# Two gated recurrences, with heads laid over the partitions and the two directions as planes

## Chip, core and metric

The kernel runs on one core of a Trainium2 chip. The metric is the device time of one launch in microseconds (us). The engines are called as the profile calls them: PE (the matrix engine; PEld is its weight load), DVE (vector), ACT (scalar), POOL and SP.

## What is computed

Two transformer blocks over 512 positions of width 1024, in fp32. The change touches the first block's mixers alone. Three mixers read one projection of the input: differential attention (a), a gated recurrence with four heads of 64 keys (b), and one with four heads of 32 keys (c). Both recurrences run forward and backward and are summed:

```python
def chunk_scan(q, k, v, log_a):
    # S_t = diag(a_t) S_{t-1} + k_t v_t^T,  o_t = S_t^T q_t, chunkwise
    ...
        cum = jnp.cumsum(ac, axis=2)
        o_inter = jnp.einsum('bhtk,bhkv->bhtv', qc * jnp.exp(cum), state)
        diff = cum[:, :, :, None, :] - cum[:, :, None, :, :]
        scores = jnp.einsum('bhtk,bhsk,bhtsk->bhts', qc, kc, decay)   # decay = exp(diff), causal
        o_intra = jnp.einsum('bhts,bhsv->bhtv', scores, vc)
        new_state = jnp.exp(last[:, :, 0, :])[..., None] * state + jnp.einsum(
            'bhsk,bhsv->bhkv', kc * jnp.exp(last - cum), vc)
...
def bidir_scan(q, k_fwd, k_bwd, v, la_fwd, la_bwd):
    fwd = chunk_scan(q, k_fwd, v, la_fwd)
    bwd = flip(chunk_scan(flip(q), flip(k_bwd), flip(v), flip(la_bwd)))
    return (fwd + bwd).astype(q.dtype)
```

In b the keys of the two directions differ (one minus the forget gate of each), in c they are the same.

## The kernel before

Positions lie on the free axis (512 columns), features on the partitions. Large matmuls run as three of a split pair: weights are cut by ACT (`WH`) and POOL (`WL`) into two parts, the input into `HHI` and `HLO`, and each tile of weights costs three matmuls of 512 columns. Each engine runs one instruction list in its given order; semaphores alone tie the lists together. For the mixers, all five lists come from one list of steps, `P.steps`. The planner's `placed` merges five streams by a start and a gap, both counted in rows of the projection stream: `projections` (25 units of weights, 8 rows each, six matmuls of 512 columns in a plain row), `decays` of b, `recurrences` (start 8, gap 1.1) and `attention` (start 75, gap 1.7). An engine picks its own part out of every step.

There are six recurrence scans. Two are c's (two heads each), four are b's (one head each). The 128 partitions of a scan hold, for each head, the forward keys and then the backward keys. So queries and keys of every head are copied by small DMAs to the partitions of both directions (`QKC`, on SP's queue, lines 669 to 676; `QKB`, on ACT's queue, `copies`). Inside a chunk of 128 positions the scores are built in eight levels. On level lv, blocks of 2m positions (m = 64 halved lv times) are cut in the middle, and only pairs across the middle are right; a mask picks them. The steps of a level:

- `differ` (DVE, line 2191): running sum of log decay less its value at the block's middle, into `DD`, 512 elements a partition
- `expo` (ACT, lines 1574 to 1578): four exponentials of 256 elements. The first two write the query's factors and take a bias from `SC` that makes one direction zero
- `scale` (DVE, line 2199): multiplies queries and keys by them, 1024 elements
- `product` (PE, line 981): keys times queries for each of four chunks, c into banks 4 and 5 (two heads of 64 rows), b into bank 4 (one head of 128 rows)
- `collect` (DVE, lines 2208 and 2213): the bank's 512 scores into `SCT`, masked from level 1 on. The next product into the bank waits for it (`free`, `holds`)

`DD` has two buffers, so `differ` of a level waits for the product two levels back. Between the levels of a scan stand the steps that carry the state from chunk to chunk: `ends` and `reach_k` (factors and keys, `KH`), `turn` (four transposes into bank 6), an eviction into `KN` by ACT, `state` (bank 6), `carry` (DVE, `ST`, lines 2241 to 2245, chain by direction and head) and `read` (bank 7, scores times values plus state times queries). The norm of an output pair then takes the step `mean` (PE, bank 6) and a logarithm on ACT that frees the bank.

Of the kernel before, what the change touches and what calls it, by code (L numbers as in the profile page):

```python
# [24 lines left out]
DECAY, RECUR, ATTEND = ((16, 2), (34, 2.2)), (8, 1.1), (75, 1.7)  # L25
LEVELS = [(r, lv) for r in range(6) for lv in range(7)]
# [57 lines left out]
def unit_order():  # L84
# [14 lines left out]
    for d, (tag, n) in enumerate(DENSE):  # L99
        if tag == "bz":  # L100
            c = []
            for h in (2 * n, 2 * n + 1):
                c += [(1792 + 64 * h, 64), (2048 + 64 * h, 64)]
# [51 lines left out]
def unit_size(u):  # L155
# [6 lines left out]
       ("sgnh", 1), ("sgnc", 1), ("fh", 1), ("bh", 1), ("fc", 1), ("bc", 1),  # L162
# [70 lines left out]
class Plan:  # L233


    def __init__(self):
# [7 lines left out]
        for u in self.units:  # L244
# [8 lines left out]
        self.slots()  # L253
        self.steps = placed((self.projections(), (0, 1)), (self.decays(0), DECAY[0]), (self.decays(1), DECAY[1]),
                            (self.recurrences(), RECUR), (self.attention(), ATTEND))
# [30 lines left out]
    def place(self):  # L286
# [3 lines left out]
        for d, (tag, n) in enumerate(DENSE):  # L290
            if d == 9:
                self.turn = 0
            self.take(four if d < 9 else [3, 5], (at[tag, n], 0), (at[tag, n], 1))
# [41 lines left out]
    def projections(self):  # L335

        late, later, copies = [], [], []
        for tag, n in DENSE:
# [14 lines left out]
            for m in range(2):  # L353
                for row in range(4):
                    r = 4 * m + row
                    step = [("nat", i, m, row // 2)] * (row % 2 == 0) if natural else [("gemm", i, m, 2 * row)]
                    yield step + beside[r] + (late if row == 1 else []) + (later if row == 2 else []) + (copies if row == 3 else [])
                late = [("evict", i, tag, n, m)]
                later = [("silu", i, tag, m)] if tag in ("cg", "bg", "bq") else []
                copies = [("copies", m)] if tag == "bq" else []  # L360
# [6 lines left out]
    def recurrences(self):  # L367
# [4 lines left out]
        box = {0: ("c", 0), 1: ("c", 1), 3: ("b", 0), 5: ("b", 1)}  # L372
# [4 lines left out]
        for r in range(6):  # L377
            for k in range(8):
                g = 7 * r + k
                one, two, three = [("product", r, k)], [], []  # L380
                if k < 7 and g + 1 < len(LEVELS):
                    two.append(("scale", *LEVELS[g + 1]))
                if k < 7 and g + 2 < len(LEVELS):
                    two.append(("differ", *LEVELS[g + 2]))
                    three.append(("expo", *LEVELS[g + 2]))
                if k == 0 and r:
                    two.insert(0, ("read", r - 1))
                elif k == 1:
                    one.append(("ends", r))
                elif k == 2:  # L390
                    three.append(("turn", r))
                elif k == 3:
                    two.append(("state", r))
                elif k == 4:
                    one.append(("carry", r))
                    one.append(("eq", r))
                elif k == 5 and r < 5:
                    one.append(("lag", r + 1))
# [2503 lines left out]
```

## Time and profile before

| | us |
|---|---|
| median of 3 runs | 2272.03 |
| lowest and highest | 2271.94, 2275.05 |
| the profiled execution | 2274.05 |
| its span in the profile | 2272.3 |

The recurrences run between about 60 and 460 us of the span. A line of the timeline is one instruction or several equal ones in a row; a matmul of plain fp32 operands is recorded as two passes, so x8 is four matmuls. A wait is the idle time of an engine just before an instruction, with what ended it. PEclk is the share of full clock granted to PE: 1.00 is 2.4 GHz, 0.50 is 1.2 GHz.

### The profile page before, as it was taken

How to read it: one execution, taken by the hardware profiler on the slowest of the kernel's cores; microseconds unless marked ns; L12 is line 12 of the kernel's file. 1: busy time of each engine (PE TensorE's matmuls, PEld its weight loads, DVE VectorE, ACT ScalarE, POOL GpSimd, SP SyncE). 2: the span in 40 equal slices, each digit the busy share in tenths (PEclk: the TensorE clock that was granted, in tenths of full speed). 3: DMA queues.
4: the chain of work that ended last, by engine and by line, in shares of the span. 5: the costliest groups of instructions: out<-in, count | busy, mean ns of one | idle time of the engine just before them, and what ended most of it. 6: DMA issues, size and time to landing. Idle time of an engine off the chain costs nothing.

```text
span 2272.3 us, 29053 instructions
## 1 busy us (share of the span) xinstructions
PE 2220.5 (98%) x11592; PEld 1848.7 (81%) x11592; DVE 1150.9 (51%) x1864; ACT 998.5 (44%) x1888; POOL 1051.0 (46%) x794
## 2 busy tenths in 40 slices
PE   7899999999999999999999999999999999999998
PEld 4788777778988888888888888878888889888887
DVE  4887777736532122477672425431534446725353
ACT  4765566654533223566632322453322336322234
POOL 2544443446454444633454445544444444554444
PEclk9999999999999999999999999999999999999999
DMA  7222233464222232321223222322222222322321
GB/s 285 93 81 106 95 119 130 157 227 181 94 93 93 93 112 93 95 75 57 75 93 111 84 102 93 111 93 93 86 100 93 75 93 78 109 93 84 104 108 58
DMA packets 42663, 239.41 MB, mean 105 GB/s; under 512 B 5024, under 2 KB 7200, under 8 KB 17184
## 3 DMA queue, kind: packets, MB, share of 16 engines
q1 hardware_dynamic: 40096, 232.28, 28.9%
q10 hardware_dynamic: 2432, 5.27, 0.8%
q8 instruction: 92, 1.51, 0.3%
q14 instruction: 43, 0.35, 0.0%
HBM read 225.99 MB, written 8.39 MB: 103 GB/s over the span
## 4 chain that ended last, share of the span: by engine, by line
PE 81%; DVE 11%; ACT 4%; POOL 1%; issue 1%; DMA 1%; DVEq 0%; SPq 0%; ACTq 0%; POOLq 0%
PE PS L741 80%; DVE DD L1890 2%; POOL WL L2641 1%; DVE TG L1896 1%; DVE SQ L1896 1%; PE PS L1165 1%; DVE SCT L2213 1%; ACT WH L1316 1%; DVE HLO L1896 1%; DVE VV L1893 0%; DVE SB L2267 0%; DVE SB L1896 0%; DVE T L1890 0%; DVE PS L1896 0%; DVE X L1890 0%
## 5 line engine op out<-in xcount | busy, mean ns | idle before, releaser
L2641 POOL TENSOR_TENSOR WL<-RAW,WH 128x512 fp32r<-128x512 f32 (+1 forms) x688 | 924.0, 1372 | 1101.0 <-ACT WH L1316 1089.7
L741 PE MATMUL PS<-HHI,WH 128*128 128x512 f32 x1488 | 596.4, 401 | 1.5 <-DVE GB L1896 1.4
L741 PE MATMUL PS<-HHI,WL 128*128 128x512 f32 x1488 | 581.9, 391 | 0.0
L741 PE MATMUL PS<-HLO,WH 128*128 128x512 f32 x1488 | 581.4, 391 | 0.0
L1316 ACT ACTIVATE WH<-RAW 128x512 fp32r<-128x512 f32 (+1 forms) x688 | 378.3, 613 | 392.3 <-PE PS L741 376.5
L741 PEld LDWEIGHTS PS<-HHI,WH 128*128 128x128 f32 x1488 | 280.6, 189 | 72.5 <-issue 10.0
L741 PEld LDWEIGHTS PS<-HHI,WL 128*128 128x128 f32 x1488 | 280.3, 188 | 59.7
L741 PEld LDWEIGHTS PS<-HLO,WH 128*128 128x128 f32 x1488 | 280.7, 189 | 56.8 <-issue 2.4
L741 PE MATMUL PS<-UF,WH 128*128 128x512 f32 (+1 forms) x832 | 224.0, 357 | 0.0
L1890 DVE TENSOR_TENSOR T<-PS,R 128x512 f32<-128x512 f32 x112 | 76.9, 690 | 218.1 <-PE PS L741 210.2
L741 PEld LDWEIGHTS PS<-UF,WH 128*128 128x128 f32 x832 | 148.3, 189 | 22.8
L741 PE MATMUL PS<-UP,WH 128*128 128x512 f32 x512 | 157.6, 389 | 0.0
L1890 DVE TENSOR_TENSOR Y<-PS,Y 128x512 f32<-128x512 f32 (+1 forms) x97 | 66.3, 686 | 170.8 <-PE PS L741 170.7
L741 PE MATMUL PS<-UF,WL 128*128 128x512 f32 (+1 forms) x416 | 148.3, 356 | 0.0
L1834 ACT ACTIVATE TG<-TG 128x512 f32<-128x512 f32 x44 | 27.8, 632 | 206.3 <-DVE TG L1896 206.3
L741 PEld LDWEIGHTS PS<-UP,WH 128*128 128x128 f32 x512 | 96.1, 188 | 20.1
L741 PE MATMUL PS<-WH,HHI 128*128 128x256 f32 (+1 forms) x320 | 110.9, 347 | 0.2 <-ACT VV L1852 0.2
L741 PE MATMUL PS<-WL,HHI 128*128 128x256 f32 (+1 forms) x320 | 108.7, 340 | 0.0
L741 PE MATMUL PS<-WH,HLO 128*128 128x256 f32 (+1 forms) x320 | 108.7, 340 | 0.0
L1896 DVE SCALAR_TENSOR_TENSOR X<-PS,MOD,X 128x512 f32<-128x512 f32 (+1 forms) x56 | 37.0, 673 | 141.0 <-PE PS L741 141.0
L1896 DVE SCALAR_TENSOR_TENSOR TG<-T,V,TG 128x511 f32<-128x511 f32 x88 | 104.1, 1183 | 3.1
L741 PE MATMUL PS<-UP,WL 128*128 128x512 f32 x256 | 99.6, 389 | 0.0
(360 smaller groups left out, 3492.7 us busy)
## 6 DMA issues: line engine op xcount, KB each, us to landing
RAW<-in_wts SPq DMA_DIRECT2D x190, 1024.0 KB, 4.8
FW<-in_wts SPq DMA_DIRECT2D x6, 1024.0 KB, 17.4
spill<-T SPq DMA_DIRECT2D x24, 256.0 KB, 3.2
RAW<-in_wts SPq DMA_DIRECT2D x8, 768.0 KB, 4.2
GT<-spill SPq DMA_DIRECT2D x20, 256.0 KB, 4.9
X<-in_xt SPq DMA_DIRECT2D x2, 1024.0 KB, 9.1
out_x<-X SPq DMA_DIRECT2D x8, 256.0 KB, 2.3
X<-in_xt SPq DMA_DIRECT2D x2, 768.0 KB, 8.1
```

The lines of the kernel that those rows point to most:

```text
L741: return e.matmul(o_, l, r, start=start, stop=stop)
L1165: t = e.transpose(PS[:, 2 + part, 128 * s:128 * s + 128], S[:, s, 128 * part:128 * part + 128], ident)
L1316: e.activation(WH[i][:, cs], RAW[i % 2][:, cs], ACT.Copy).then_inc(*up("w_hi", ("w_hi", i, p)))
L1834: e.activation(G, G, ACT.Gelu_apprx_tanh).then_inc(*up("a_ev", ("gelu", name, j)))
L1890: return e.tensor_tensor(o_, a, b, f)
L1896: return e.scalar_tensor_tensor(out=o_, in0=a, scalar=s, in1=b, op0=f1, op1=f2)
L2213: t = e.copy_predicated(SCT[n][:, :].rearrange("p (c t) -> p c t", c=4), mk, PS[:, b, :].rearrange("p (c t) -> p c t", c=4))
L2641: return e.tensor_tensor(o_, a, b, f)
```

## The change

The partitions of a scan now hold heads alone, and the two directions are two planes of the free axis. Scan 0 is all four heads of c (32 rows each, `PAIRS` 2: its products come in two pairs), scans 1 and 2 are two heads of b each (64 rows, one pair). The running sums lie in `Am` as two planes, backward and forward. On a level each position is a query in one direction and a key in the other, so `differ` writes both halves by two instructions of 512 elements, and all of `DD` is used: no factor is set to zero, and one product serves both directions. Level 7, the diagonal, now uses the sum of both keys. Each product writes banks 4 and 5; `turn` writes banks 4 and 5, `state` bank 4, `mean` bank 5. The DMAs for `QKC` and `QKB` are gone. The c scan keeps start 8 and gap 1.1, the two b scans start at row 65 with gap 2.2.

```diff
-DECAY, RECUR, ATTEND = ((16, 2), (34, 2.2)), (8, 1.1), (75, 1.7)
-LEVELS = [(r, lv) for r in range(6) for lv in range(7)]
+DECAY, RECUR, ATTEND = ((16, 2), (34, 2.2)), ((8, 1.1), (65, 2.2)), (75, 1.7)
+LEVELS = [(r, lv) for r in range(3) for lv in range(8)]
+PAIRS = (2, 1, 1)
...
-        for m in range(2):
-            q.wait_ge(*at(("ev", U["cqk", 0], m)))
-            for n in range(8):
-                r, c = 64 * (n // 2 % 2) + 32 * (n % 2), 32 * (n // 2)
-                t = e.dma_start(QKC[r:r + 32, n // 4, m, :], T0[m][c:c + 32, :])
...
         # tensor_program: product
-            for n in range(len(heads)):
-                free(product_bank(r, n))
+            for i in range(2):
+                free(4 + i)
             for c in range(4):
                 cs = slice(128 * c, 128 * c + 128)
-                for n, (r0, nr, _, _) in enumerate(heads):
-                    t = mm(PS[:, product_bank(r, n), cs], both[r0:r0 + nr, 1, cs], both[r0:r0 + nr, 0, cs], True, True)
+                for i in range(2):
+                    rs = slice(nr * (2 * j + i), nr * (2 * j + i) + nr)
+                    t = mm(PS[:, 4 + i, cs], D[rs, 1, cs], D[rs, 0, cs] if lv < 7 else planes[rs, 0, cs], True, True)
...
         # tensor_program: turn
-            free(6)
-            for c in range(4):
-                t = e.transpose(PS[:, 6, 128 * c:128 * c + 128], KH[:, 128 * c:128 * c + 128], ident)
+            for d in range(2):
+                free(4 + d)
+                for k in range(3):
+                    t = e.transpose(PS[:, 4 + d, 128 * k:128 * k + 128], KH[:, d, 128 * k:128 * k + 128], ident)
...
         # scalar_program: expo
-            e.activation(Q[:, :, 0:m], K[:, :, 0:m], ACT.Exp, scale=-s, bias=SC[:, b[0]:b[0] + 1])
-            e.activation(Q[:, :, m:2 * m], K[:, :, m:2 * m], ACT.Exp, scale=s, bias=SC[:, b[1]:b[1] + 1]).then_inc(*up("a_mix", ("expo_q", r, lv)))
-            q.wait_ge(*at(("expo_q", r, lv)))
-            e.activation(K[:, :, 0:m], K[:, :, 0:m], ACT.Exp, scale=-s)
-            e.activation(K[:, :, m:2 * m], K[:, :, m:2 * m], ACT.Exp, scale=s).then_inc(*up("a_mix", ("expo", r, lv)))
+            e.activation(halves(D, lv, 0), halves(D, lv, 0), ACT.Exp, scale=-s)
+            e.activation(halves(D, lv, 1), halves(D, lv, 1), ACT.Exp, scale=s).then_inc(*up("a_mix", ("expo", r, lv)))
...
         # vector_program: differ, scale
-            tt(blocks(level(r, lv)[:, 1, :], lv), blocks(Am[:, :], lv), ref, SUB).then_inc(*up("d_mix", ("differ", r, lv)))
+            tt(halves(D, lv, 0), halves(sums, lv, 0), middle, SUB)
+            tt(halves(D[:, ::-1, :], lv, 1), halves(sums, lv, 1), middle, SUB).then_inc(*up("d_mix", ("differ", r, lv)))
...
-            tt(D, both, D, MUL).then_inc(*up("d_mix", ("scaled", r, lv)))
+                if r == 0:
+                    t = tt(D, planes, D, MUL)
                 else:
+                    tt(halves(D, lv, 0), halves(planes[:, 0:2, :], lv, 0), halves(D, lv, 0), MUL)
+                    t = tt(halves(D, lv, 1), halves(planes[:, 0:3:2, :], lv, 1), halves(D, lv, 1), MUL)
...
         # vector_program: carry
-            for n, (r0, nr, _, _) in enumerate(heads):
-                hf = nr // 2
-                for d, (s, c) in enumerate(((slice(r0, r0 + hf), [0, 1, 2, 3]), (slice(r0 + hf, r0 + nr), [3, 2, 1, 0]))):
-                    e.memset(ST[s, c[0], :], 0.0)
-                    e.tensor_copy(ST[s, c[1], :], S3[s, c[0], :]).then_inc(*up("d_mix", ("chain", r, n, d, 1)))
+            e.tensor_copy(ST[:, 0:6:5, :], S[:, 0:6:5, :]).then_inc(*up("d_mix", ("chain", r, 0)))
+            for k in (1, 2):
+                q.wait_ge(*at(("chain", r, k - 1)))
+                stt(ST[:, k, :], ST[:, k - 1, :], TD[:, k:k + 1], S[:, k, :], MUL, ADD)
+                n = 5 - k
+                t = stt(ST[:, n, :], ST[:, n + 1, :], TD[:, n + 2:n + 3], S[:, n, :], MUL, ADD)
```

The order of the carry on DVE, first scan. Before, the last two of its four chains (two heads, two directions), and the decays' step after them (`G`, of b's first half):

```order
L2241 MEMSET ST 32x64
L2242 COPY ST<-PS 32x64
L1896 SCALAR_TENSOR_TENSOR ST<-ST,TD,PS 32x64 x2
L2241 MEMSET ST 32x64
L2242 COPY ST<-PS 32x64
L1896 SCALAR_TENSOR_TENSOR ST<-ST,TD,PS 32x64 x2
L1896 SCALAR_TENSOR_TENSOR G_90<-G_90,LB,G_91 128x512 x2
```

After, the same place: the whole carry is two rows, and it stands right behind `differ` and `collect` of the same level; b's second half of decays stands around it:

```order
L1867 TENSOR_TENSOR ZB<-ZB,G_91 128x1024
L1867 TENSOR_TENSOR DD_107<-Am 128x512
L1867 TENSOR_TENSOR DD_107<-Am 128x2x256
L2189 COPY_PREDICATED SCT_110<-MASK,PS 128x1024
L2209 COPY ST<-PS 128x2x64
L1873 SCALAR_TENSOR_TENSOR ST<-ST,TD,PS 128x64 x4
L2276 COPY VB<-PS 128x512
L1873 SCALAR_TENSOR_TENSOR G_90<-G_90,LB,G_91 128x512 x2
```

What moved: sixteen rows' worth of chains of 32 partitions became five instructions over all 128, and the carry came behind a `collect`.

PE, from the transposes of the first scan to the next product. Before:

```order
L1003 MATMUL PS<-V,KH 128x128 x4
L741 MATMUL PS<-HHI,WH_66 128x512
L741 MATMUL PS<-HLO,WH_66 128x512
L741 MATMUL PS<-HHI,WL_68 128x512
L741 MATMUL PS<-HHI,WH_66 128x512
L741 MATMUL PS<-HLO,WH_66 128x512
L741 MATMUL PS<-HHI,WL_68 128x512
L741 MATMUL PS<-DD_107 128x128 x8
```

After:

```order
L994 MATMUL PS<-V,KH 128x128 x6
L732 MATMUL PS<-HHI,WH_66 128x512
L732 MATMUL PS<-HLO,WH_66 128x512
L732 MATMUL PS<-HHI,WL_68 128x512
L732 MATMUL PS<-HHI,WH_66 128x512
L732 MATMUL PS<-HLO,WH_66 128x512
L732 MATMUL PS<-HHI,WL_68 128x512
L732 MATMUL PS<-DD_107 128x128 x8
```

The distance is the same six matmuls; but the transposes now lie in the product's own banks, so the last row waits for the eviction into `KN` between them.

ACT, the exponentials of a level and that eviction. Before:

```order
L1574 ACTIVATE DD_106<-DD_106,SC 128x64x4
L1575 ACTIVATE DD_106<-DD_106,SC 128x64x4
L1577 ACTIVATE DD_106<-DD_106 128x64x4
L1578 ACTIVATE DD_106<-DD_106 128x64x4
L1607 ACTIVATE KN<-PS 128x512
```

After, with the decays' `G` and the eviction of b's queries ahead of it:

```order
L1531 ACTIVATE G_89<-ZB 128x1024
L1533 ACTIVATE G_89<-G_89 128x1024
L1645 ACTIVATE QKB<-PS 128x512
L1564 ACTIVATE DD_108<-DD_108 128x256x2
L1565 ACTIVATE DD_108<-DD_108 128x256x2
L1595 ACTIVATE KN<-PS 128x768
```

Four exponentials became two of twice the size, and `KN` grew from 512 to 768 elements.

## Rows read from the trace of the kernel before

**Rows 1.** Busy time by engine in two stretches, granted clock, DMA; first the columns
```profile
core 0: us, PE busy (x) PEld busy (x) DVE busy (x) ACT busy (x) POOL busy (x), PEclk, DMA share, GB/s
60.00:180.00 120.00, 107.64 (x775) 92.45 (x775) 101.87 (x145) 84.70 (x152) 59.57 (x35) 0.94 0.26 86
180.00:460.00 280.00, 268.23 (x1503) 215.36 (x1502) 213.93 (x342) 170.75 (x355) 119.30 (x78) 0.99 0.35 125
```

**Rows 2.** PE's waits, 60 to 180 us: total, times, longest
```profile
PE PS L741 <- DVE SCT L2213: 10.2, 2, 6.1
PE PS L741 <- DVE Am L2183: 2.1, 1, 2.1
```

**Rows 3.** PE's waits, 180 to 460 us, the longest total
```profile
PE PS L741 <- DVE SCT L2213: 3.1, 3, 2.5
```

**Rows 4.** Timeline of PE after its longest wait: start, us, instruction, idle before
```profile
113.75 2.08 PE L741 MATMUL PS<-DD 64*128 64x128 f32 x16 [6.08 <-DVE SCT L2213]
...
118.91 0.63 PE L741 MATMUL PS<-HLO,WH 128*128 128x512 f32 x1
119.34 0.58 PE L741 MATMUL PS<-HHI,WL 128*128 128x512 f32 x1
```

**Rows 5.** Timeline of PE around a product of c
```profile
133.89 0.39 PE L741 MATMUL PS<-HHI,WL 128*128 128x512 f32 x1
134.21 1.16 PE L741 MATMUL PS<-DD 64*128 64x128 f32 x16
135.30 0.50 PE L741 MATMUL PS<-HHI,WH 128*128 128x512 f32 x1
135.64 0.39 PE L741 MATMUL PS<-HLO,WH 128*128 128x512 f32 x1
```

**Rows 6.** Timeline of PE around a product of b
```profile
272.32 0.39 PE L741 MATMUL PS<-HLO,WH 128*128 128x512 f32 x1
272.54 0.39 PE L741 MATMUL PS<-HHI,WL 128*128 128x512 f32 x1
272.77 1.05 PE L741 MATMUL PS<-DD 128*128 128x128 f32 x8
273.58 0.48 PE L741 MATMUL PS<-HHI,WH 128*128 128x512 f32 x1
273.89 0.40 PE L741 MATMUL PS<-HLO,WH 128*128 128x512 f32 x1
```

**Rows 7.** Timeline of PE, state times queries, one of c and one of b
```profile
137.92 1.09 PE L741 MATMUL PS<-KH,ST 64*64 64x128 f32 x16
...
390.88 1.04 PE L741 MATMUL PS<-KH,ST 128*64 128x128 f32 x8
```

**Rows 8.** DVE's groups by form, 60 to 460 us: busy, mean ns | idle before
```profile
L1890 DVE TENSOR_TENSOR DD<-QKB,DD 128x1024 f32<-128x1024 f32 x28 | 41.7, 1489 | 4.1 <-ACT DD L1578 4.1
L2213 DVE COPY_PREDICATED SCT<-MASK,PS 128x512 f32<-128x512 uint8 x56 | 39.4, 730 | 2.5 <-PE PS L741 2.4
L1890 DVE TENSOR_TENSOR DD<-Am,ZB 128x512 f32<-128x512 f32 x28 | 29.1, 1039 | 9.9 <-PE PS L741 8.0 <-ACT Am L1564 1.8
```

**Rows 9.** ACT's groups by form, 60 to 460 us
```profile
L1574 ACT ACTIVATE DD<-DD,SC 128x256 f32<-128x256 f32 x42 | 21.4, 510 | 48.0 <-DVE DD L1890 47.9
L1577 ACT ACTIVATE DD<-DD 128x256 f32<-128x256 f32 x42 | 17.8, 425 | 1.3
L1629 ACT ACT_TABLE_LOAD x7 | 9.0, 1283 | 0.1
L1563 ACT ACTIVATE Am<-ZB 64x512 f32<-64x512 f32 x4 | 2.5, 619 | 0.0
```

**Rows 10.** Timeline of DVE, the first scan's carry: its first instruction, and the next step
```profile
103.25 0.11 DVE L2241 MEMSET ST<- 32x64 f32 x1
...
107.23 2.20 DVE L1896 SCALAR_TENSOR_TENSOR G<-G,LB,G 128x512 f32<-128x512 f32 x2
```

**Rows 11.** Timeline of PE, the first scan's transposes
```profile
94.05 0.60 PE L1003 MATMUL PS<-V,KH 128*128 128x128 f32 x4
```

**Rows 12.** Timeline of ACT, the first scan's eviction into KN
```profile
95.83 0.57 ACT L1607 ACTIVATE KN<-PS 128x512 f32<-128x512 f32 x1
```

More of the change, by code:

```diff
@@ L335, in projections @@
     def projections(self):
-        late, later, copies = [], [], []
+        late, later = [], []
         for tag, n in DENSE:
@@ L376, in recurrences @@
         yield [("scale", 0, 0), ("expo", 0, 1)]
[L377 to L381, printed above, removed]
+        for g, (r, k) in enumerate(LEVELS):
+            for j in range(PAIRS[r]):
+                last = j + 1 == PAIRS[r]
+                one, two, three = [("product", r, k, j)], [], []
+                if (r, k) == (2, 0):
+                    two.append(("read", 1, 0))
+                if j == 0 and g + 1 < len(LEVELS):
@@ L391, in recurrences @@
                     three.append(("turn", r))
[L392 to L395, printed above, removed]
+                elif last and k == 4:
                     one.append(("eq", r))
-                elif k == 5 and r < 5:
-                    one.append(("lag", r + 1))
-                if k == 1:
-                    three.append(("reach_k", r))
-                if k == 5:
-                    two.append(("reach_q", r))
@@ L403, in recurrences @@
-                if k > 3 and r - 1 in box:
-                    three.append(("norm", *box[r - 1], k - 4))
-                two.append(("collect", r, k))
+                    three.append(("state", r))
+                    three.append(("carry", r))
+                elif last and k == 5:
+                    two.append(("reach_q", r))
+                    if r < 2:
+                        three.append(("lag", r + 1))
+                elif last and (r, k) == (0, 7):
+                    one.append(("read", 0, 0))
@@ new lines, in recurrences @@
+                two.append(("collect", r, k, j))
+                for at_, step in {(1, 0): ((one, 0), (three, 1), (three, 2)), (1, 1): ((one, 3),), (1, 2): ((one, 4), (three, 5), (three, 6)),
+                                  (1, 3): ((two, 7),), (2, 0): ((three, 8),), (2, 1): ((three, 9), (three, 10)),
+                                  (2, 2): ((two, 11),)}.get((r, k), ()):
+                    at_.append(("norm", *(("c", 0), ("c", 1), ("b", 0))[step // 4], step % 4))
+                if (r, k) == (1, 1):
+                    three.append(("read", 0, 1))
@@ L1013, in state @@
+            for n in range(6):
+                d, k = divmod(n, 3)
+                for i in range(128 // nr):
+                    t = mm(PS[nr * i:nr * i + nr, 4, 64 * n:64 * n + 64], KN[:, d, 128 * k + nr * i:128 * k + nr * i + nr],
+                           vals[:, k + d, vc + 64 * i:vc + 64 * i + 64], True, True)
             t.then_inc(*up("psum", ("state", r)))
-            holds(6, ("carry", r))
-        def read(r):
-            _, _, heads, vals, _, _, _, _, _ = scan(r)
+            holds(4, ("carry", r))
@@ L1595, in ends_q @@
         def ends_q(r):
+            s = scan(r)[5]
             q.wait_ge(*at(("turn", r)))
[L1598 removed]
+            e.activation(KH[:, 0, :], FWD[:, 128:512], ACT.Exp, scale=s)
+            for c in range(3):
                 cs = slice(128 * c, 128 * c + 128)
[L1600 removed]
+                t = e.activation(KH[:, 1, cs], BWD[:, cs], ACT.Exp, scale=-s, bias=SC[:, 12 + c:13 + c])
             t.then_inc(*up("a_mix", ("eq", r)))
```

318 lines of the change are left out of this document (137 added, 181 removed).

## The prediction, made before the run

> **What bounds the kernel now.** I read the busy time by stretch first, then who PE waited for, then the timeline at those waits. PE is the bound: in the recurrences it is busy 107.6 of 120 us and 268.2 of 280 us [rows 1], and outside them the change touches nothing. So only three things can give time: the 24.1 us that PE stands idle there (12.4 and 11.8), the clock it loses after a stand, and PE's own work. The waits say whose fault the idle time is. In the first stretch it is DVE alone: 10.2 us for `collect` (line 2213), 2.1 us for a small memset [rows 2]. DVE is busy 101.9 of 120 us there [rows 1], so it is not one slow step but a queue that is full. In the second stretch `collect` is 3.1 us [rows 3], and the rest of the 11.8 us is spread over waits of attention's and the norms' steps, mostly on DVE, which is busy 76% there [rows 1].
>
> A stand costs more than itself. After the wait of 6.08 us the matmuls of 512 columns follow each other at 0.43 us (118.91 to 119.34) [rows 4], where elsewhere it is 0.23 us (272.32 to 272.54) [rows 6]: the clock is at 1.2 GHz in place of 2.4. That lasts to 119.6 or so, 6 us of work at half pace, some 2.6 us lost. The mean clock of the two stretches, 0.94 of 120 us and 0.99 of 280 us [rows 1], makes 7.2 and 2.8 us of clock not granted; part of it fell into idle time. I take 8 us as the price of the clock.
>
> **PE's own work.** The cost of a product is what it adds to the pace of its neighbours. A product of c: from the matmul ahead of it to the second one behind, 135.64 - 133.89 = 1.75 us, less two paces of 0.227 us: 1.30 us, for eight matmuls on 64 rows [rows 5]. One of b: 273.89 - 272.54 = 1.35, less 0.45: 0.90 us, for four matmuls on 128 rows [rows 6]. So sixteen passes on half the rows take 1.09 us where eight on all rows take 0.81: pairs on two row halves run at the same time, and the entry and exit cost a little more. Before there are 16 products of c and 32 of b: 16 x 1.30 + 32 x 0.90 = 49.6 us. After there are 32, all of eight matmuls in pairs: 32 x 1.30 = 41.6 us. That is 8 us less. Half of them are on quarters of the rows (32), which no row shows; at worst the two quarters do not overlap, and a product costs twice the four matmuls of b, 1.80 us: 16 x 0.5 = 8 us more, and this gain is gone. At best they cost what the halves cost; the order gives PE only two quarters at a time, so not less. I take 1.30, since the mechanism is the same.
>
> The Trainium skill ("TensorEngine Tiling (Array Packing)", Restrictions and Gotchas) says that different row tiles cannot access the same PSUM bank simultaneously. State times queries of c does just that, two row halves into bank 7, and its sixteen passes take 1.09 us where b's eight on all rows take 1.04 [rows 7]: the trace does not agree for this case. By the page's rule each of the four new reads would be some 1.4 us longer, 5.6 us in all; by the row it is nothing.
>
> The rest of PE: 24 transposes become 18, four of them took 0.60 us [rows 11], so 0.6 to 0.7 us less with their entries. States: 32 matmuls in six groups become 48 in three, reads: 64 in six groups become 80 in four. Matmuls in pairs cost about 0.13 us each (1.09 us for eight [rows 7]), and a group's entry and exit is about 0.2 us: 16 more matmuls of state at 0.08 (half the columns) against three entries and the unpaired four of b, about -0.8 us; reads 4 x 2.8 against 2 x 2.25 + 4 x 2.1, about -1.8 us. Sum of PE's own work: -8 - 0.7 - 0.8 - 1.8 = **-11.3 us**. All of this is on the path, since PE is.
>
> **DVE.** `scale`: 42 instructions of 1024 elements at 1.49 us [rows 8] (c's are alike) become 7 of 1024 and, in b, 28 of 512 at 1.04 us, plus three additions of 512: 62.6 becomes 10.4 + 29.1 + 3.1, 20 us less. `differ`: 42 of 512 before, 42 of 512 after, at 1.04 us [rows 8]: nothing. `collect`: 64 of 512 at 0.73 us [rows 8] become 32 of 1024; per element it must read as much, and only the fixed part is saved, about 2.5 us. `carry`: the four chains of c take 107.23 - 103.25 = 3.98 us [rows 10], b's two chains half; 2 x 4 + 4 x 1.9 = 15.6 us become three times one copy and four multiply-adds, some 1.3 us: 11.6 us less. `ends`: six instructions' worth of small work each becomes one, 2.5 us less. Together 36 us of 315.8 [rows 1]. In the first stretch it is 10 (scale) + 1.3 + 6.7 + 0.9, 19 us of 101.9: DVE's share falls from 85 to 70%.
>
> **ACT.** `expo`: 42 x (2 x 0.51 + 2 x 0.42) = 78 us [rows 9] become 21 x 2 of 512 elements without a bias, 0.62 us by the copy of that size [rows 9]: 26 us, 52 less. The factors of `KH` and the copies of `Am` save another 14. ACT had 255 us [rows 1], so it was no bound; the gain is that a level's chain, `differ`, `expo`, `scale`, is a microsecond shorter, and that ACT's queue is seldom late. POOL's `reach` shrinks by a quarter. The small DMAs stood on queues that nobody waited for: nothing.
>
> **What becomes of the waits.** The 6.08 us wait ends a stretch in which DVE has no idle time; it now has at least 6 us less to do there (a scale and four carry chains), so I take this wait as gone. The 4.1 us one has the decays of b's second half ahead of it, 10 us in a row on DVE. They still stand there, so 1 to 3 us stay. The memset is gone with its 2.1 us. In the second stretch `collect` mostly goes, and of the 8.7 us of others a third, as DVE falls to about 70%.
>
> Three kinds of wait are new, because bank 6 is given up. (1) After `turn`, the next product waits for `KN`: before, `KN` ended at 96.40 [rows 12], 1.8 us behind the transposes' end [rows 11], and six matmuls at 0.23 are 1.4 us; with a wider `KN` and a shorter `expo` ahead some 0.8 us in c, nothing in b, where more stands between. Behind the waiting product everything on PE is queued, the projections too. (2) After `state`, the next product waits for the carry, 1.3 us and DVE's queue; `state` itself waits for the `collect` of its own level. I take 3.5 us in c (with the rest of the 4.1 us above) and 1 us in each b scan. The bound from above is what the trace shows: `state` was done at 99.3 and the carry at 107.2 [rows 10], 8 us later. (3) After `mean` in bank 5 the next product waits for the logarithm, a table load of 1.28 us [rows 9] and 0.7 us, with twelve matmuls or 2.7 us as cover: 0.7 us each for three outputs. Together 8.3 us new, 4.3 us old: 12.6 in place of 24.1, **-11.5 us**. Of the clock's 8 us I take half, as short waits remain: **-4 us**.
>
> Sum: -11.3 - 11.5 - 4 = -26.8 us. The profiled execution took 2274.05 us, 2.0 us above the median of the runs; the sum on the execution is 2247.3, and on the median 2245.2. I say **2245**.
>
> **Rivals.** *All cover holds*: no new wait shows and DVE is never late. Then 11.3 + 24.1 less about 2 + 8 = 41 us go: 2231. For it speaks DVE's share of 70%; against it the lumps of the decays. *The waits only change their name*: the order decides, not the load, and each wait removed comes back at a shared bank. Then PE's own work is left: 2261. *Quarters do not pair*: the change does not do on PE what it does for the halves: 2245 + 8 = 2253. *Slower*: the shared banks. Nine places (`KN`, carry and logarithm, three each) put PE behind another engine's queue. The trace shows 1.8 and 8 us for the first two. If each costs over 4 us net, that is 36 us and eats all that the change gives (11.3 + 17 + 8); at 5.5 us it is 49.5 us, and with the clock's half pace after the longer ones 2286. Against it speaks that both queues get shorter, and that in b the steps stand twice as far apart.
>
> **Chances.** Forecast 0.55, all cover 0.15, name change 0.13, quarters 0.07, slower 0.06, and 0.04 that it cancels within 0.2%. The range 2230 to 2262 takes in the first four. A measurement can tell about 0.2%, 4.5 us: faster 0.89, same 0.05, slower 0.06.
>
> **What would show it.** Products of 16 passes on 32 and 64 rows at 1.1 us with 1.30 us added; PE idle 12 to 13 us between 60 and 440 us, in waits of under 3 us; the wait of 6 us gone; at most two stretches at 1.2 GHz; DVE near 280 and ACT near 190 us over the recurrences; waits of a product on `KN`, `ST` and the logarithm, each near 1 us. It is wrong if the waits at banks 4 and 5 add up to over 15 us, if the quarters' products cost 1.8 us, or if DVE's instructions with two planes and short blocks run longer than those of the same size before.

## The result, and the profile after

The changed kernel takes 2276.93 us (median of 18 runs, 2275.04 to 2278.47), the one before beside it 2272.43 us (18 runs, 2269.92 to 2275.07): a ratio of 1.0018, with an interval of 1.0012 to 1.0025. That is 4.5 us slower: small, just the size that the prediction called the least that can be told, but with an interval that does not reach 1. 2245 was forecast, and 2276.9 lies outside the range of 2230 to 2262. The profiled execution took 2276.7 us. Of all executions reported here one is left out, of `before_split`: it ran at a mean granted clock of 0.75 and took 2754.97 us.

Busy time by stretch comes first, as in [rows 1]: PE, PEld, DVE, ACT and POOL, the granted clock, DMA.

```profile
60.00:180.00 120.00, 111.40 (x800) 95.58 (x800) 95.85 (x94) 64.91 (x96) 62.02 (x38) 0.95 0.20 69
180.00:460.00 280.00, 260.28 (x1541) 201.18 (x1541) 193.14 (x278) 128.38 (x244) 107.92 (x74) 0.95 0.35 125
```

Over 60 to 460 us, ACT went from 255.5 to 193.3 us, as forecast (190). DVE went from 315.8 to 289.0, 27 us less where 36 were forecast (280), and in the first stretch it lost only 6.0 us where 19 were: its share is 80% there, not 70%. In the first stretch PE stands idle 8.6 us instead of 12.4. In the second, where the prediction let most waits of before go and added small ones, it stands idle 19.7 us instead of 11.8, and the granted clock there fell from 0.99 to 0.95. Who PE waited for, 60 to 180 us and then 180 to 460 (total, times, longest), against [rows 2, 3]:

```profile
PE PS L732 <- DVE SCT L2189: 6.4, 4, 2.7
PE PS L732 <- DVE ST L1873: 1.4, 1, 1.4
```
```profile
PE PS L732 <- DVE T L1873: 4.9, 2, 2.9
PE PS L1046 <- DVE SB L1873: 4.0, 1, 4.0
PE PS L732 <- DVE SCT L2189: 3.7, 1, 3.7
PE PS L732 <- DVE SQ L1873: 3.0, 1, 3.0
PE PS L732 <- ACT T L1608: 3.0, 1, 3.0
```

The 6.1 us wait and the memset's 2.1 are gone. In their place stand many waits of 2 to 4 us, and in the second stretch most of them are not on the recurrences at all: `SB` is the attention's tile, `T` the norms', and `SQ` a sum that DVE makes for the modulation. The timeline of PE at three of the longer ones shows the price of each (start, duration, instruction, idle before it):

```profile
238.43 1.12 PE L1046 MATMUL PS<-V,SB 128*128 128x128 f32 x4 [3.96 <-DVE SB L1873]
239.20 0.78 PE L732 MATMUL PS<-HHI,WH 128*128 128x512 f32 x1
239.78 0.63 PE L732 MATMUL PS<-HLO,WH 128*128 128x512 f32 x1
240.20 0.63 PE L732 MATMUL PS<-HHI,WL 128*128 128x512 f32 x1
```
```profile
376.41 1.85 PE L732 MATMUL PS<-V,SQ 128*128 128x1 f32 x8 [2.98 <-DVE SQ L1873]
378.12 1.52 PE L994 MATMUL PS<-V,KH 128*128 128x128 f32 x6
```
```profile
146.87 0.88 PE L732 MATMUL PS<-VC,KN 128*32 128x64 f32 x48 [2.68 <-DVE SCT L2189]
149.18 2.08 PE L732 MATMUL PS<-DD 32*128 32x128 f32 x16 [1.43 <-DVE ST L1873]
```

Behind the wait at 238.43, matmuls of 512 columns follow each other at 0.42 us (239.78 to 240.20), where [rows 6] have 0.23: 1.2 GHz in place of 2.4. The product at 149.18 takes 2.08 us, where 1.16 is the rule, as in [rows 4]. Over four short stretches the granted clock reads as follows:

```profile
112.00:132.00 20.00, 17.74 (x100) 13.67 (x100) 15.54 (x20) 11.70 (x21) 10.77 (x8) 0.91 0.30 106
144.00:160.00 16.00, 11.89 (x132) 11.06 (x131) 12.64 (x17) 7.05 (x11) 4.43 (x4) 0.79 0.21 68
232.00:248.00 16.00, 12.04 (x50) 9.07 (x49) 13.32 (x24) 4.93 (x10) 6.55 (x5) 0.79 0.36 131
372.00:384.00 12.00, 9.02 (x37) 7.62 (x37) 4.51 (x6) 3.91 (x8) 1.36 (x1) 0.72 0.52 193
```

To see what went where, I took the same four numbers from every trace: PE's idle time between 56 and 600 us (604 for before_tight, whose head starts later); the stretches at 1.2 GHz in it; what they cost (half of the part of them that was not idle); and the start of the first matmul of the mlp's head, which is preceded by an idle 0.53 us in every kernel. The last of them less idle time and clock is PE's own work, with a constant that is the same for all. The kernels below "after" are the experiments of the next section.

| kernel | median us | idle | at 1.2 GHz (stretches) | clock lost | head starts | own work |
|---|---|---|---|---|---|---|
| before | 2272.4 | 25.5 | 20.5 (5) | 9.8 | 591.0 | 555.7 |
| after | 2276.9 | 32.0 | 44.4 (10) | 20.4 | 593.4 | 541.0 |
| norm_late | 2264.8 | 27.2 | 27.3 (6) | 12.5 | 580.4 | 540.7 |
| state7 | 2270.3 | 31.5 | 27.3 (8) | 13.7 | 587.0 | 541.8 |
| scale_one | 2275.0 | 34.4 | 37.5 (8) | 16.4 | 591.4 | 540.6 |
| both | 2258.5 | 23.7 | 13.7 (3) | 6.7 | 573.7 | 543.3 |
| both_shift | 2256.2 | 22.1 | 23.9 (5) | 11.1 | 575.2 | 542.0 |
| both_coll | 2255.4 | 23.1 | 13.7 (3) | 5.8 | 571.8 | 542.9 |
| both_attn | 2257.9 | 22.7 | 27.3 (6) | 13.5 | 577.7 | 541.5 |
| before_split | 2276.2 | 27.5 | 20.5 (5) | 9.5 | 593.5 | 556.5 |
| before_late | 2271.9 | 24.6 | 27.3 (5) | 11.0 | 590.7 | 555.1 |
| before_tight | 2286.4 | 35.5 | 37.5 (7) | 14.4 | 604.0 | 554.1 |

So the change does save PE's own work, and more than forecast: 555.7 to 541.0, 14.7 us. It pays back 6.5 us in waits and 10.6 in clock, 2.4 us more than it saved. Of the profiled execution's 2.7 us more span, 2.4 are there by the head of the mlp. The column "own work" agrees within 2.7 us for the changed kernel and the seven made from it, and within 2.4 for the kernel before and the three made from it, so the split can be trusted to about that.

The columns after the median are of one execution each, and the clock's depends on more than the edits. In both, behind a wait of 1.89 us at 146.5 us, there is no stretch at 1.2 GHz; in both_shift and both_attn, behind waits of 1.91 and 1.88 us at the same place, there is one of 6.8 us, 3.4 us lost. The profiled executions of these two are 2.2 and 3.0 us above their medians. That the change costs clock at all is in every execution: the mean granted clock is 0.989 to 0.991 in the 18 of the changed kernel and 0.993 to 0.996 in those of the kernel before it.

### The profile page after: what moved, and what is told of

Same layout as the page of the kernel before. It is cut to its first block, busy times and chain, and to the rows that moved or that the text cites. A ratio compares the mean times of both kernels' runs of the same rounds, so it can differ in the third digit from the quotient of the medians.

```text
span 2275.0 us, 28817 instructions
## 1 busy us (share of the span) xinstructions
PE 2216.9 (97%) x11650; PEld 1837.9 (81%) x11650; DVE 1125.6 (49%) x1747; ACT 937.6 (41%) x1722; POOL 1042.6 (46%) x794
## 4 chain that ended last, share of the span: by engine, by line
PE 84%; DVE 9%; ACT 4%; POOL 1%; issue 1%; DMA 1%; ACTq 0%; DVEq 0%; SPq 0%; POOLq 0%
PE PS L732 83%; DVE DD L1867 2%; POOL WL L2607 1%; PE PS L1162 1%; DVE SQ L1873 1%; ACT WH L1313 1%; DVE HLO L1873 1%; DVE VV L1870 0%; DVE SCT L2189 0%; DVE TG L1873 0%; DVE PS L1873 0%; DVE X L1867 0%; DMA X<-in_xt 0%; DVE SB L1873 0%; ACT SB L1630 0%
## 5 line engine op out<-in xcount | busy, mean ns | idle before, releaser
L732 PEld LDWEIGHTS PS<-UF,WH 128*128 128x128 f32 x832 | 148.3, 189 | 22.7
```

Source lines behind the costliest of these rows:

```text
L732: return e.matmul(o_, l, r, start=start, stop=stop)
```

## Why PE waits: three theories, and the runs that tell them apart

**Theory 1, the head of DVE's line at the norms.** In the order before, the square, the mean, the logarithm with the multiply, and the copy of a norm stood one level apart. In the changed order, for three of the norms, the mean (step 1) and step 2, which is ACT's logarithm and exponential and then DVE's multiply, are due in one entry. DVE reaches its multiply before ACT has begun, and stands at it with everything behind it. DVE's timeline ahead of the wait at 238.43 shows it:

```profile
223.05 0.75 DVE L1873 SCALAR_TENSOR_TENSOR SQ<-RAW,CC,SQ 128x512 f32<-128x512 f32 x1
230.54 0.75 DVE L1873 SCALAR_TENSOR_TENSOR T<-PS,V,R 128x512 f32<-128x512 f32 x1 [6.74 <-ACT R L1620]
231.21 0.74 DVE L1873 SCALAR_TENSOR_TENSOR SQ<-RAW,CC,SQ 128x512 f32<-128x512 f32 x1
231.87 0.68 DVE L2235 CUSTOM_DVE_ANT_0 SB<-PS,MC 128x512 f32<-128x512 f32 x1
...
236.75 1.63 DVE L1873 SCALAR_TENSOR_TENSOR SB<-SB,SC,SB 128x512 f32<-128x512 f32 x1
```

ACT's, in the same time:

```profile
226.49 1.28 ACT L1617 ACT_TABLE_LOAD   x1
227.78 0.69 ACT L1617 ACTIVATE R<-PS,EPSC 128x512 f32<-128x512 f32 x1
228.49 1.28 ACT L1620 ACT_TABLE_LOAD   x1
229.78 0.72 ACT L1620 ACTIVATE R<-R,EPSC 128x512 f32<-128x512 f32 x1
```

DVE stands 6.74 us for `R`. The attention's logits (line 2235) are queued behind it, ACT's softmax behind those, then the division and `SB` again on DVE, and at the end PE's four transposes, 3.96 us late. The chain crosses three engines before PE notices.

**Theory 2, the shared bank of the states.** `state` writes into bank 4, which the level's own product holds until DVE has collected it. At 146.87 PE waits 2.68 us for that, and then 1.43 us more for the carry.

**Theory 3, DVE in lumps.** b's `scale` is two instructions in place of one, and a level's collect stands behind `scale` and `differ`. DVE ahead of the wait at 376.41, under GpSimd's `WL`:

```profile
368.72 3.48 DVE L1867 TENSOR_TENSOR DD<-QKB,DD 128x512 f32<-128x512 f32 x2
372.13 2.38 DVE L1867 TENSOR_TENSOR DD<-Am 128x512 f32<-128x512 f32 x2
374.43 1.29 DVE L2189 COPY_PREDICATED SCT<-MASK,PS 128x1024 f32<-128x1024 uint8 x1
375.62 0.73 DVE L1873 SCALAR_TENSOR_TENSOR SQ<-RAW,CC,SQ 128x512 f32<-128x512 f32 x1
```

### norm_late: DVE's part of the norms behind ACT's

DVE's and GpSimd's part of each norm becomes a step of its own (4), one entry later for the three outputs inside the recurrences; for b's last and the attention's it stays in the entry of step 2. The copy of step 3 moves one or two entries later with it. By the traces PE's order stays the same. DVE's multiply goes behind seven instructions at the second of the three norms, among them the attention's logits, and behind three at the third; at the first it passes nothing. ACT's copies (`OC`, `OB`) move too, and no run moves them alone.

```diff
-{(1, 0): ((one, 0), (three, 1), (three, 2)), (1, 1): ((one, 3),), (1, 2): ((one, 4), (three, 5), (three, 6)), ...
-at_.append(("norm", *(("c", 0), ("c", 1), ("b", 0))[step // 4], step % 4))
+{(1, 0): ((one, 0), (three, 1), (three, 2)), (1, 1): ((one, 4), (three, 3)), (1, 2): ((one, 5), (three, 6), (three, 7)), ...
+at_.append(("norm", *(("c", 0), ("c", 1), ("b", 0))[step // 5], step % 5))
...
-            if step == 2:
+            if step == 4:
                 q.wait_ge(*at(("r", kind, n)))
```

> The changed kernel, with the vector part of each norm (DVE's multiplication by 1/rms and what follows it) one or two steps of its stream behind ACT's logarithm and exponential. Theory 1, head of line: DVE's queue stands at that multiplication until ACT has gone through two table loads (DVE idle before T 23.6 + 7.5 us between 60 and 480 us), the softmax of attention queued behind it is late, and PE waits for SB or T. Then DVE's idle time before T falls below 15 us, PE's waits for T and SB (11.9 us) fall by 6 us or more, the stretches at 1.2 GHz lose two, and the time falls by 6 to 12 us, to 2265 to 2271. Theory 2, shared banks 4 and 5: PE's waits are at the state and the products, nothing of them goes, time within 3 us of the changed kernel (2274 to 2280). Theory 3, DVE's work in lumps: the same as theory 2.

Measured: 2264.84 us (2263.80 to 2267.34), 0.9973 of the kernel before (0.9961 to 0.9984), 12.1 us under the changed kernel. The same piece of DVE's timeline now reads:

```profile
224.68 0.69 DVE L2235 CUSTOM_DVE_ANT_0 SB<-PS,MC 128x512 f32<-128x512 f32 x1 [0.63 <-PE PS L732]
...
229.98 0.75 DVE L1873 SCALAR_TENSOR_TENSOR T<-PS,V,R 128x512 f32<-128x512 f32 x1 [1.99 <-ACT R L1620]
```

The logits stand ahead of the norm's multiply, begin at 224.7 instead of 231.9, and PE's wait there is 0.52 us instead of 3.96. DVE still waits for `R`, but nothing that is urgent stands behind it. Theory 1 holds: the time fell to just under its range, though one of its signs was weaker (DVE's waits for `R` fell to 16.9 us, not below 15). By the table 4.8 us of the gain are idle time and 7.9 are clock. At the wait of 238.43 alone 3.4 us of idle time and a stretch with 2.5 us lost are gone. But two stretches, 3.4 us lost in all, are also gone behind waits that kept their length (1.98 and 1.97 us at 290 and 284 us, 1.89 and 1.87 at 471 and 458), so part of the 12 us is where such stretches happen to fall.

### state7: the states in a bank of their own

```diff
-            free(4)
+            free(7)
...
-            holds(4, ("carry", r))
+            holds(7, ("carry", r))
```

(and bank 7 in the matmuls and in the carry's read.)

> The changed kernel, with the state matmuls of a scan in bank 7 in place of bank 4, so that the state no longer waits for the collect of its level and the next product no longer for the carry. Theory 2, shared banks: the waits of the state (2.7 and 3.7 us) and of the product behind the carry (1.4 us) go, with the half clock that follows two of them, together 8 to 12 us: 2265 to 2269. Theory 1, head of line at the norms: the 7.8 us of these waits go or turn up at the next product's collect, the rest of PE's waits stays, time falls by 0 to 5 us. Theory 3, DVE in lumps: the state no longer waits but the next product does, for the same collect: under 3 us.

Measured: 2270.31 us (2268.07 to 2272.01), ratio 0.9990 (0.9981 to 0.9999), 6.6 us under the changed kernel: less than the 8 to 12 us that theory 2 gave and more than the 0 to 5 of theory 1. The waits of 2.68 and 3.74 us at the two states are gone. PE's idle time fell only from 32.0 to 31.5: at 147 us a wait of 1.87 and at 402 us one of 1.89 come instead, and a wait for the attention's norm at 355 us grew from 2.88 to 4.47. But the stretches at 1.2 GHz fell from 44.4 to 27.3 us, the clock lost from 20.4 to 13.7.

Only 1.0 us of these 6.7 is at a state: two stands in a row, 2.68 and 1.43 us with 0.88 us of matmuls between them, became one, and the stretch behind them went from 6.8 to 3.4 us. The rest is at places whose waits the edit did not shorten. Behind the 3.96 us at 235 us the stretch is 3.4 us where it was 6.8; behind the 2.93 us at 372 us likewise; behind the 2.97 us at 344 and the 1.87 at 464 us there is none where there was one. The gain is in all eleven executions (mean granted clock 0.991 to 0.993, against 0.989 to 0.991), so it is real. That the states' own waits are what brings it is not shown.

### scale_one and before_split: the lumps

One takes b's second `scale` instruction away in the changed kernel, and leaves b's backward keys out of its scores by that; the other puts it into the kernel before.

```diff
-                    tt(halves(D, lv, 0), halves(planes[:, 0:2, :], lv, 0), halves(D, lv, 0), MUL)
-                    t = tt(halves(D, lv, 1), halves(planes[:, 0:3:2, :], lv, 1), halves(D, lv, 1), MUL)
+                t = tt(D, planes[:, 0:2, :], D, MUL)
```
```diff
-            tt(D, both, D, MUL).then_inc(*up("d_mix", ("scaled", r, lv)))
+                for hf in range(2):
+                    a, b = [... the blocks' half hf of D and of both ...]
+                    t = tt(a, b, a, MUL)
```

> The changed kernel, with b's scale as one instruction of 1024 elements in place of two of 512 (it takes the forward keys for both directions, so the backward keys are left out of b's scores on levels 0 to 6). Theory 3, DVE in lumps: under POOL's weight splits two short instructions take 3.48 us where one long took 2.3, fourteen times; then DVE loses some 10 us of work (28 x 1.17 against 14 x 1.5), the waits at 376 and 397 us shrink by over 1 us each, time falls by 4 to 8 us. Theories 1 and 2: time falls by under 3 us, since the waits come from the order and not from DVE's load.

> The kernel before, with each of the 28 scales of b as two instructions of 512 elements (same result). Theory 3, DVE in lumps: DVE gets 28 x (2 x 1.17 - 1.49), 24 us more work, where it is the bound of the waits, and the time rises by 6 us or more, to over 2278. Theories 1 and 2: the time rises by under 4 us.

Measured: scale_one 2274.99 us (2268.55 to 2276.30), 1.9 us under the changed kernel, ratio to before 1.0007 (0.9998 to 1.0016); before_split 2276.22 (2275.43 to 2277.49), ratio 1.0019 (1.0010 to 1.0028), 3.3 us above the kernel before beside it (2272.91). The second is clear of noise; the first isn't, as its interval meets the changed kernel's (1.0012 to 1.0025). So the split has a price of some 2 to 4 us, which the prediction did not have: there 20 us less of DVE's `scale` were counted at nothing either way, being off the path. The waits at the states and norms do not hang on it: in scale_one they are 2.67, 3.65 and 3.99 us (2.68, 3.74 and 3.96 in the changed kernel).

Both runs test theory 3 less hard than was meant. DVE's groups over 60 to 460 us, in before_split:

```profile
L1890 DVE TENSOR_TENSOR DD<-QKB,DD 128x512 f32<-128x512 f32 x56 | 51.8, 965 | 5.5 <-ACT DD L1578 5.3
L1890 DVE TENSOR_TENSOR DD<-Am,ZB 128x512 f32<-128x512 f32 x28 | 24.7, 882 | 8.4 <-PE PS L741 6.6 <-ACT Am L1564 1.7
```

Splitting added 10.1 us to `scale` (41.7 in [rows 8]), not 24, while `differ` lost 4.4 (29.1 in [rows 8]); all of DVE went from 315.8 to 316.6 us only. In scale_one `scale` lost 9.4 us, `differ` gained 7.7, and all of DVE went from 289.0 to 285.9. So they show what the number of instructions costs, and not what 24 us of load would.

### before_tight and before_late: the same edits in the kernel before

If theory 1 is right, the order before must become slow in the same way when its norms are drawn together. PE's order is the same in this kernel. By the traces DVE's multiply stands 4, 8 and 15 instructions earlier at the three norms (not two to four, as the expectation has it), and ACT's table loads, logarithm and exponential move up with it.

```diff
-                if k > 3 and r - 1 in box:
-                    three.append(("norm", *box[r - 1], k - 4))
+                if r - 1 in box:
+                    three += [("norm", *box[r - 1], n) for n in {4: (0,), 5: (1, 2), 6: (3,)}.get(k, ())]
```

> The kernel before with the norms of its recurrences drawn together as the change has them: the mean and the step with logarithm, exponential and multiply in one step, the square and the copy where they would then fall; nothing else is changed (TensorE's row order is the same, VectorE's multiply stands two to four instructions earlier). If the head of VectorE's line at the norms is what the change added, it is slower by 3 to 10 us: 2275 to 2282, with VectorE's waits for R up from 14.2 by 8 us or more. If the banks or the lumps of VectorE's work are the cause, it stays at 2271 to 2274.

> The kernel before with the norm's edit alone: VectorE's and GpSimd's part of each norm as a step of its own behind ScalarE's. In the kernel before the mean already stands a level ahead of ScalarE's logarithm, but VectorE's multiply in the same step as ScalarE's two table loads, and VectorE waited 14.2 us for R. If the cost in the changed kernel came from drawing the mean and that step together (23.6 us of waits for R there), little is to be had here: 2270 to 2273. If every place where VectorE reaches the multiply in the same step costs alike, it gains 3 to 8 us: 2264 to 2269.

Measured: before_tight 2286.36 us (2284.82 to 2286.98), ratio 1.0058 (1.0045 to 1.0070), 12.9 us slower than the kernel before beside it, where theory 1 gave 3 to 10. before_late 2271.91, ratio 0.9996 (0.9987 to 1.0005): no change. DVE and then PE of before_tight:

```profile
245.98 0.75 DVE L1896 SCALAR_TENSOR_TENSOR T<-PS,V,R 128x512 f32<-128x512 f32 x1 [7.18 <-ACT R L1632]
246.64 0.74 DVE L1896 SCALAR_TENSOR_TENSOR SQ<-RAW,CC,SQ 128x512 f32<-128x512 f32 x1
...
248.82 1.63 DVE L1896 SCALAR_TENSOR_TENSOR SB<-SB,SC,SB 128x512 f32<-128x512 f32 x1
```
```profile
250.51 1.11 PE L1049 MATMUL PS<-V,SB 128*128 128x128 f32 x4 [8.53 <-DVE SB L1896]
```

The same signature, in a kernel without a single one of the change's other parts: DVE 7.2 us at the norm's multiply, the softmax's last steps behind it (the logits are ahead of it here), and a wait of 8.5 us at the attention's transposes. With the stretch of 10.2 us at 1.2 GHz around it (2.6 us lost), this one place has 11.2 of the 12.9 us; in the kernel before PE has no wait there. And DVE's waits for `R` over 60 to 480 us, in before, after, before_tight and before_late:

```profile
DVE T L1896 <- ACT R L1632: 14.2, 4, 5.1
```
```profile
DVE T L1873 <- ACT R L1620: 23.6, 4, 7.9
```
```profile
DVE T L1896 <- ACT R L1632: 22.6, 4, 7.2
```
```profile
DVE T L1898 <- ACT R L1634: 7.3, 2, 4.2
```

Up by 8.4 us costs 12.9 us; down by 6.9 us brings nothing. The total of an idle time on DVE is no measure: in the kernel before, the longest of the four (5.13 us, at 249.72) stands behind the softmax and the collect of its level, and no step of the attention is among the next three behind it.

### both, and the start moved by one: do the gains add?

> The changed kernel with both edits at once: VectorE's and GpSimd's part of each norm as a later step of its own, and the states with their carries in bank 7. If the two causes are separate (the head of VectorE's line at the norms, and the states that wait for a collect in bank 4), their gains of 12.1 and 6.6 us add: 2258.2, range 2255 to 2262, with TensorE's waits of 2.71 and 3.7 us at the states and of 3.96 us at the transposes of the attention gone together, and less than 25 us at 1.2 GHz between 56 and 600 us. If both only move one shared slack (a stream that is late waits at its next partner anyway), the gains overlap and it comes at 2262 to 2265, no better than the norm's edit alone.

> The kernel with both edits, and the start of the second stream of recurrences one step later (66 in place of 65), so that everything from the second scan on meets the stages' own steps and the attention elsewhere; no work is changed. If the time lies in the two named causes, which are gone here, it stands within 2 us of the kernel with both edits. If it lies in where short waits happen to fall (and what stretches at 1.2 GHz they bring), it may go 3 to 8 us either way, and the gains of the two edits have that uncertainty on them too.

Measured: both 2258.53 us (2256.38 to 2260.16), ratio 0.9935 (0.9923 to 0.9948). The sum of the two gains had given 2258.2, and overlapping gains 2262 to 2265. The gains of the two edits add, in time; where the clock's part of them comes from is as open as above. both_shift (the second stream's start, 65, is 66): 2256.20 (2254.36 to 2258.41), 2.3 us less, with other waits at other places (5.2 us at one of them). That is between the under 2 us and the 3 to 8 us that were expected. So how the streams happen to meet is worth 2 us or so by this one shift, under what the two edits bring. PE's waits in both, 60 to 180 us and 180 to 460:

```profile
PE PS L732 <- DVE SCT L2189: 5.6, 4, 2.3
```
```profile
PE PS L732 <- DVE T L1873: 7.2, 3, 4.1
PE PS L1046 <- DVE SB L1873: 3.4, 3, 1.9
PE PS L732 <- DVE SQ L1873: 1.9, 1, 1.9
```

### both_coll and both_attn: the waits that are left

```diff
+                two.append(("collect", r, k, j))
                 if last and g + 2 < len(LEVELS) and LEVELS[g + 2][1] < 7:
                     two.append(("differ", *LEVELS[g + 2]))
...
-                two.append(("collect", r, k, j))
```
```diff
-            late = [[("norm", "a", h, n)] + [("norm", "a", h, 4)] * (n == 2) for n in range(4)]
+            late = [[("norm", "a", h, n)] for n in (0, 1, 2, 4, 3)]
```

> The kernel with both edits, and in every entry of the recurrences VectorE's collect ahead of the differ of the level after next (in place of behind it): the collect, for which the next product waits, no longer stands behind 2.4 to 3.5 us of other work. If the lump in front of the collect is what the waits of 2.28 us (118 us) and 1.89 us (146.5 us) at products of c, and of 1.86 us (362 us) at a product of b, still measure, most of those 6 us and part of their time at 1.2 GHz go: 2251 to 2255 from 2258.5. If the collect then only stands at the head of VectorE's line before TensorE has made its product, and what is behind it (differ, and through it ScalarE's exponential) comes late, it stays within 2 us or is slower.

> The kernel with both edits, and the same edit for the norms of the attention and the last one of b: VectorE's part one entry behind ScalarE's. TensorE still waits 4.09 us at 344.7 us and 1.98 us at 279.3 us for transposes behind VectorE, which idled 4.28 us for SS. If the head of the line at a norm costs wherever it stands, 2 to 6 us go: 2253 to 2257. If here the norm's own result is what TensorE waits for (its transposes follow at once), moving VectorE's part behind other work gains nothing or loses: 2258 to 2261.

Measured: both_coll 2255.36 us (2253.11 to 2256.80), ratio 0.9922 (0.9908 to 0.9935), 3.2 us under both; both_attn 2257.94 (2256.74 to 2260.90), 0.6 us under both, which is nothing. PE's waits for the collect over 60 to 460 us, in both_coll:

```profile
PE PS L732 <- DVE SCT L2189: 3.2, 3, 1.4
```

They fell from 5.6 to 3.2 us, by moving the urgent instruction ahead of the one that can wait; 1.4 us at `KN` and 1.4 more behind a step of the modulation (`MOD`, 1.7) are new. The time came down by the least that was expected, and by little more than the shift of a start alone brings. The wait of 4.1 us at 344.7 us in both did not go with both_attn, where it is 4.0, and is 5.1 in both_coll. The expectation takes it for transposes; it is the attention's next products with the values, whose bank (2) is held until DVE has multiplied the attention's norm:

```profile
344.70 1.62 PE L732 MATMUL PS<-WT,VA 128*128 128x128 f32 x6 [4.09 <-DVE T L1873]
```

ACT in both shows what is in front of it:

```profile
338.32 0.21 ACT L1572 ACTIVATE TD<-SC 128x8 f32<-128x8 f32 x1 [4.36 <-DVE SC L1870]
338.44 0.97 ACT L1578 ACTIVATE KH<-Am,SC 128x128 f32<-128x128 f32 x3
339.32 0.51 ACT L1579 ACTIVATE KH<-Am 128x384 f32<-128x384 f32 x1
339.84 1.28 ACT L1617 ACT_TABLE_LOAD   x1
```

ACT stands 4.36 us for `ends`' sum from DVE, with the norm's logarithm behind it, and DVE then stands 4.28 us for the norm. It looks like the same fault on the other engine; an edit of that order wasn't tried.

## Why the prediction was wrong

**What held.** PE is the bound, and its own work fell: 14.7 us by the table, 11.3 forecast. Products on quarters pair like those on halves. A product of c on 32 rows, in the changed kernel:

```profile
84.34 0.39 PE L732 MATMUL PS<-HHI,WL 128*128 128x512 f32 x1
84.66 1.16 PE L732 MATMUL PS<-DD 32*128 32x128 f32 x16
85.75 0.50 PE L732 MATMUL PS<-HHI,WH 128*128 128x512 f32 x1
86.09 0.40 PE L732 MATMUL PS<-HLO,WH 128*128 128x512 f32 x1
```

86.09 - 84.34 = 1.75, less two paces of 0.227: 1.30 us, to the digit what [rows 5] gave for halves; b's, at 230.05 to 231.80, the same. The rival in which quarters don't pair is out. State times queries of c, on row quarters into bank 7 alone, takes 1.53 us for 24 passes (182.72), no slower a pass than the 1.09 us for sixteen of [rows 7], so the 5.6 us that the prediction priced for reads into one bank did not come. ACT's load fell as forecast (193). What gave own work 3.4 us more than forecast isn't shown; 2.7 is what the column is good for. `KN` cost nothing in place of 0.8 us, and the logarithm in bank 5 nothing in place of 2.1: no product waited for either. The wait behind the decays of b's second half, 4.1 us before, is the 2.68 us at c's state now, inside the 1 to 3 us left for it.

**What failed: the step "What becomes of the waits".** It went by load. "As DVE falls to about 70%", a third of the second stretch's other waits was to go. DVE did fall, to 69% there, and the idle time of PE rose from 11.8 to 19.7 us. The change also moves the norms' steps together; the prediction went through the banks that the change shares, but costed the moved norm at nothing, and did not name what is queued on DVE behind its multiply: the attention's logits. This alone is 12.1 us of the 31.9 that are between forecast and result, by norm_late; before_tight gives 12.9 for it in the other kernel. In the first stretch the load itself was wrong: DVE lost 6.0 us where 19 were taken. Two numbers that lead to it do not hold by themselves either: of 8.7 us of other waits two thirds are 5.8 us, not the 4.3 in its sum, so its own figures give -10 and not -11.5 us; and b's `scale` halves were priced by the mean of `differ` (1.04 us), where they took 1.17. And the wait of 6.08 us, taken as gone, came back as 1.16 and 2.26 us for the collect, at 109 and 118 us. [Rows 9] had the table load of 1.28 us, two of which stand in that chain.

**The term mis-sized: the states.** 5.5 us were given to the state and carry (3.5 in c, 1 in each b). The waits were 2.68 and 1.43 in c (3.5 forecast, the rest of the old wait included), 3.74 in one scan of b (1 forecast) and none in the other: 7.8 us. The edit that takes them away brings 6.6 us of time, nearly all of it clock, and most of that clock at other places, for which no cause is shown. The rival of the shared banks named three kinds of wait, and only the one at the carry came, for 1.4 us in c; the longer ones are of the state for its collect.

**The clock.** "Of the clock's 8 us I take half": the cost rose from 9.8 to 20.4 us, so this term has the wrong sign, by 14 us. It was taken to fall, since only short waits were to remain. They did, more of them, and short ones were enough: nine of the ten stretches at 1.2 GHz stand at a wait of 1.9 to 4 us, and the stretches at c's state and the one of before at its wait of 6.1 us lost about the same, 2.7 and 3.0 us. The length of a wait does not decide it alone: 3.04 us at 152 us in before_late and 2.97 us at 344 us in state7 brought no stretch, 1.98 us at 290 us in the changed kernel did. The gains of norm_late and state7 both contain the clock, so this term isn't a third cause beside those two.

**The sum.** Forecast less 27 us; own work gave 3.4 more than its term of 11.3. Waits +6.5 in place of -11.5, clock +10.6 in place of -4: 32.6 us the other way. The balance, 29.2 us, is the 26.8 that were forecast and the 2.4 by which the mlp's head starts later. This is by the profiled executions; the one of before was 1.6 us above its median, so the medians are 4.5 us apart and not 2.7. With both edits in, both stands at 2258.5: waits -1.8 and clock -3.1 against before. That is close to the rival "the waits only change their name" (2261), and even there some 10 us of the forecast's gain in waits do not come: by these runs the order decides; what more load by itself would cost isn't tested. The 2 to 4 us of the split `scale` are in that. What is left open is the rest of the waits' forecast, of which the 4 to 5 us at the attention's values is the largest single wait.

## What to carry to other kernels

When a change moves a step, list for each engine what is queued behind the instruction that will wait, and follow it until the bounding engine. A share of busy time says nothing of this: with DVE's down from 76 to 69% PE's waits there rose by 8 us. Put the consumer's half of a two-engine step a step behind the producer's, and the instruction that the bounding engine waits for ahead of those that only prepare a later level. Then add the clock to each wait: here most waits of 2 to 4 us were followed by 1.5 to 3.4 us of lost clock, so a short one cost well over its length. And before a gain is put down to the waits that an edit removes, look whether the clock came back at those waits or elsewhere.

## What the runs showed of the hardware

Two things are worth keeping. First, two matmuls on row quarters of 32 cost what two on halves of 64 cost, 1.16 us for sixteen passes and 1.30 us added to the pace, although only two of the four quarters work at a time; a row tile of half the size is no faster. Second, how long an instruction of DVE takes depends on where it stands: `scale` on 512 elements takes 1.28 us for two (218.87) where POOL is idle, and 3.48 us for two (368.72) while POOL makes `WL` (from 368.21 on, 5.15 us for three); its mean is 1.17 us each. So an instruction's mean can't be carried over to another order. Splitting b's 28 instructions of 1024 elements in the kernel before added 0.44 us each (2 x 0.965 - 1.489), 10.1 us together. DVE's whole load over 60 to 460 us rose by only 0.8 us, in part since b's `differ` went from 1.04 to 0.88 us, and the kernel took 3.3 us more.
